# Fourteen weight slabs of an attention loop as rounded part and remainder, with reordered norms and loads

## The reference

```python
h = rms_norm(x, norm1_g[l])
z = h @ w_in[l]                                   # 1024 x 5808
(cq, ckv, kpe, gq, gk, gv, glr, gr, su, gates) = split_in(z)
o_a = mla_mixer(cq, ckv, kpe, ...)                # attention, 8 heads, two blocks of 128 queries
o_b = gla_mixer(gq, gk, gv, glr, gr, ...)         # gated linear attention
o_c = s5_mixer(su, ...)                           # y = gelu(y); y * sigmoid(y @ w_glu + b_glu)
g = sigmoid(gates + gate_b[l]).reshape(B, L, 3, D)
merged = (g[:, :, 0] * (o_a @ w_br_mla[l]) + g[:, :, 1] * (o_b @ w_br_gla[l])
          + g[:, :, 2] * (o_c @ w_br_s5[l]))
x = x + merged @ w_out[l]
h2 = rms_norm(x, norm2_g[l])
x = x + square(relu(h2 @ w_ff1[l])) @ w_ff2[l]
```

## Time and profile before

| | |
|---|---|
| median of three runs | 1526.87 us |
| profiled execution | 1527.37 us |
| its span | 1525.6 us |
| PE busy | 1479.9 us (97%) |
| PE weight loads (beside PE) | 1313.6 us (86%) |
| VectorE (DVE) busy | 739.4 us (48%) |
| ScalarE (ACT) busy | 685.2 us (45%) |
| GpSimd (POOL) busy | 862.4 us (57%) |
| mean granted TensorE clock | 0.997 of 2.4 GHz |
| loads | 234 MB, mean 154 GB/s |

### The profile page before, as it was taken

How to read it: one execution, slowest core, us unless ns; L and a number is a source line. 1 busy time by engine, 2 the same in 40 slices (tenths; PEclk the granted TensorE clock), 3 DMA queues, 4 the chain that set the end, 5 groups by cost and what they waited for, 6 DMA issues and landing times.

```text
span 1525.6 us, 23985 instructions
## 1 busy us (share of the span) xinstructions
PE 1479.9 (97%) x9775; PEld 1313.6 (86%) x9775; DVE 739.4 (48%) x1407; ACT 685.2 (45%) x1024; POOL 862.4 (57%) x364
## 2 busy tenths in 40 slices
PE   7999999999999999999999999999999999899998
PEld 6977778889898897777788888989999989799997
DVE  5978865421112697886442121128993454311112
ACT  5644222554444564422255443454445645643444
POOL 5710000878888671000086778868885536688886
PEclk9999999999999999999999999999999999999999
DMA  7633343656566563333465677656664443556664
GB/s 196 174 92 83 97 110 111 200 154 187 185 187 185 157 166 88 96 97 97 124 195 156 183 217 219 186 151 184 188 183 125 127 123 107 156 165 183 188 184 138
DMA packets 321490, 234.46 MB, mean 154 GB/s; under 512 B 9382, under 2 KB 304837, under 8 KB 321380
## 3 DMA queue, kind: packets, MB, share of 16 engines
q1 hardware_dynamic: 321380, 232.93, 52.4%
HBM read 231.82 MB, written 1.09 MB: 153 GB/s over the span
## 4 chain that ended last, share of the span: by engine, by line
PE 83%; ACT 4%; issue 4%; POOL 4%; DVE 2%; DMA 2%; SPq 0%; DVEq 0%; POOLq 0%; ACTq 0%
PE ps L678 18%; PE ps L1948 14%; PE ps L1064 7%; PE ps L1065 7%; PE ps L1066 7%; PE ps L1931 5%; PE ps L1932 5%; PE ps L1933 5%; POOL w_lo L1288 4%; DMA raw<-in_w_in_dram 1%; PE ps L1139 1%; ACT w_hi L1322 1%; PE ps L1176 1%; PE ps L2068 1%; PE ps L2082 1%
## 5 line engine op out<-in xcount | busy, mean ns | idle before, releaser
L1288 POOL TENSOR_TENSOR w_lo<-raw,w_hi 128x1024 fp32r<-128x1024 f32 (+1 forms) x206 | 490.5, 2396 | 508.2 <-ACT w_hi L1322 507.0
L746 POOL TENSOR_TENSOR w_lo<-raw,w_hi 128x1024 fp32r<-128x1024 f32 x154 | 371.7, 2421 | 144.2 <-ACT w_hi L768 142.6
L1322 ACT ACTIVATE w_hi<-raw 128x1024 fp32r<-128x1024 f32 (+1 forms) x206 | 217.5, 1058 | 239.1 <-PE ps L678 81.7
L1064 PE MATMUL ps<-h_hi,w_hi 128*128 128x256 f32 x864 | 246.3, 285 | 1.4 <-DVE h_lo L929 1.3
L1065 PE MATMUL ps<-h_lo,w_hi 128*128 128x256 f32 x864 | 244.3, 283 | 0.0
L1066 PE MATMUL ps<-h_hi,w_lo 128*128 128x256 f32 x864 | 244.2, 283 | 0.0
L1931 PE MATMUL ps<-h_hi,w_hi 128*128 128x256 f32 (+1 forms) x816 | 232.5, 285 | 4.9 <-DVE h_lo L1568 3.4
L1932 PE MATMUL ps<-h_lo,w_hi 128*128 128x256 f32 (+1 forms) x816 | 230.6, 283 | 0.0
L1933 PE MATMUL ps<-h_hi,w_lo 128*128 128x256 f32 (+1 forms) x816 | 230.5, 283 | 0.0
L768 ACT ACTIVATE w_hi<-raw 128x1024 fp32r<-128x1024 f32 x154 | 161.9, 1058 | 144.2 <-PE ps L1066 71.9
L1948 PE MATMUL ps<-hN,raw 128*128 128x256 f32 x768 | 174.9, 383 | 0.0
(11 more groups left out here) (327 smaller groups left out, 2363.1 us busy)
## 6 DMA issues: line engine op xcount, KB each, us to landing
raw<-in_w_in_dram SPq DMA_DIRECT2D x160, 512.0 KB, 3.9
raw<-in_w_ff_dram SPq DMA_DIRECT2D x128, 512.0 KB, 4.0
raw<-in_w_ffn_in_dram SPq DMA_DIRECT2D x44, 512.0 KB, 3.9
raw<-in_w_ffn_out_dram SPq DMA_DIRECT2D x22, 512.0 KB, 3.4
raw<-in_w_out_dram SPq DMA_DIRECT2D x16, 512.0 KB, 3.4
raw<-in_w_br_gla_dram SPq DMA_DIRECT2D x8, 512.0 KB, 3.5
raw<-in_w_br_mla_dram SPq DMA_DIRECT2D x8, 512.0 KB, 3.6
raw<-in_w_br_s_dram SPq DMA_DIRECT2D x8, 512.0 KB, 4.1
```

The costliest lines, as they stand in the source:

```text
L746: nc.gpsimd.tensor_tensor(out=w_lo[(NS * L + i) % RING][:, 0:kt * n], in0=raw[(NS * L + i) % RING][:, 0:kt * n], in1=w_hi[(NS * L + i) % R ...
L1064: MM(out, w[0], x[0], start=first_k, stop=False, skip_group_check=skip)
L1288: nc.gpsimd.tensor_tensor(out=w_lo[(NS * l + i) % RING][:, 0:kt * n], in0=raw[(NS * l + i) % RING][:, 0:kt * n], in1=w_hi[(NS * l + i) % R ...
L1322: A_(w_hi[(NS * l + i) % RING][:, 0:kt * n], raw[(NS * l + i) % RING][:, 0:kt * n], ACT.Copy)\
```

## The change

Fourteen slabs per layer (tiles 16 to 23 of the gates, the four of w_br_gla, the GLU's two; `in_loop`) are now rounded part and remainder too, but in buffers of their own (`wb_hi`, `wb_lo`, three each) and with the remainder on VectorE instead of GpSimd. Their right-hand sides are split as well: hN into g_hi and g_lo, rr into r_hi and r_lo, the gelu's output into u_hi and u_lo, each rounded by ScalarE and subtracted by VectorE. `raw` is let go by `wl_ok`, when the remainder is there. The square inside gelu moves from VectorE to ScalarE.

Besides: `norm_rows` takes the whole row of b = 1 at once; roundings move (`prep(I_FF + 1)` ahead of the norms, `prep(2)` ahead of a wait, one slab fewer in the second block's middle norms); the tables' load moves from behind slab I_FF + 12 to behind I_FF + 1; the bias bands come in eight loads of three rows' sets instead of four of six.

```diff
+    I_LS = I_GATE + 16
+    N_LS = I_BRA - I_LS
...
-            if b == 0:
...
+            act.wait_ge(*ready(2 * b + 1))
+            A_(sqt[:, b, :], xt[:, b, :], ACT.Square, accum_out=c[2]).then_inc(norm_sq.s, 2)
+            act.wait_ge(norm_sq.s, norm_sq(l, n + 2))
+            A_(c[3], c[2], ACT.Ln, scale=1.0 / DM, bias=C("eps")).then_inc(norm_ln.s, 2)
...
-            n = 6
+            n = 3
             band = bass.AP(scratch.tensor, 384 * n * part, [[1, P], [384, n], [1, 2 * P]])
...
-                        prep(slab + 3)
+                        prep(slab + 2)
...
-            h_rounded(1, "g_pre_ffn", J_FF + 3)
+            h_rounded(1, "g_pre_ffn", J_FF + 2)
...
+                    elif in_loop(j):
+                        sp.wait_ge(wl_ok.s, wl_ok(l, j - I_LS + 1))
                     else:
                         sp.wait_ge(used.s, used(l, j + 1))
...
-                    if i == I_FF + 12 and l == DEPTH - 1:
+                    if i == I_FF + 1 and l == DEPTH - 1:
+                        sp.wait_ge(used.s, used(l, I_OUT))
                         second_tables(sp)
...
-                    if i - I_FF in (28, 32, 36, 40) and l == DEPTH - 1:
+                    if i - I_FF in range(28, 52, 3) and l == DEPTH - 1:
...
                 norm_rows(act, A_, l, 0, 1, x_ready)
+                prep(2)
                 act.wait_ge(cols_ok.s, cols_ok(l, 1))
...
+                def loop_hi(k):
+                    i = I_LS + k
+                    if not 0 <= k < N_LS:
+                        return
+                    act.wait_ge(load_sem(l, i), load_count(l, i))
+                    if k == 2:
+                        act.wait_ge(gl_ok.s, gl_ok(l, 2))
+                    if k >= 3:
+                        act.wait_ge(used.s, used(l, i - 2))
+                    n = SLABS[i][2] * SLABS[i][4]
+                    A_(flat(i, wb_hi), raw[(NS * l + i) % RING][:, 0:n], ACT.Copy).then_inc(wh_ok.s, 1)
+
+                def gates_hi(half):
+                    act.wait_ge(of_ok.s, of_ok(l, 2))
+                    A_(g_hi[:, 4 * half:4 * half + 4, :], hN[:, 4 * half:4 * half + 4, :], ACT.Copy).then_inc(gh_ok.s, 1)
...
                 exps(0)
+                gates_hi(0)
                 for n in range(8):
...
+                    loop_hi(2 * n - 1)
                     if n < 6:
                         gate(EARLY + n)
+                    if n == 0:
+                        loop_hi(0)
                     if n + 1 < 8:
                         exps(n + 1)
+                    if n == 0:
+                        gates_hi(1)
+                    else:
+                        loop_hi(2 * n)
+                    if n == 4:
+                        act.wait_ge(y_ps.s, y_ps(l, 7))
+                        A_(r_hi, rr, ACT.Copy).then_inc(rh_ok.s, 1)
+                    if n == 5:
+                        act.wait_ge(y_rd.s, y_rd(l, 4))
+                        A_(sq[:, 4:8, :], sq[:, 0:4, :], ACT.Square, scale=float(np.sqrt(0.044715))).then_inc(ge_sq.s, 1)
...
-                prep(I_FF)
+                prep(I_FF + 1)
                 for b in range(NT):
                     norm_rows(act, A_, l, 1, b, lambda i: (x_mid.s, x_mid(l, i + 1)))
-                    prep(I_FF + 1)
...
+                def loop_lo(k):
+                    if not 0 <= k < N_LS:
+                        return
+                    i = I_LS + k
+                    n = SLABS[i][2] * SLABS[i][4]
+                    dve.wait_ge(wh_ok.s, wh_ok(l, k + 1))
+                    tt(flat(i, wb_lo), raw[(NS * l + i) % RING][:, 0:n], flat(i, wb_hi), ALU.subtract).then_inc(wl_ok.s, 1)
...
                     if h:
                         rotate(h)
+                    if n == 1:
+                        for half in range(2):
+                            dve.wait_ge(gh_ok.s, gh_ok(l, half + 1))
...
                     if n == 6:
-                        link(V.tensor_scalar(g_, g_, 0.044715, 1.0, ALU.mult, ALU.add))
-                        tt(g_, g_, y_, ALU.mult).then_inc(ge_in.s, 1)
+                        dve.wait_ge(ge_sq.s, ge_sq(l, 1))
+                        stt(g_, g_, 1.0, y_, ALU.add, ALU.mult).then_inc(ge_in.s, 1)
...
                     normalise(n)
+                    loop_lo(2 * n - 2)
...
+                    if n:
+                        loop_lo(2 * n - 1)
...
-                        product32(l, I_GATE + i, pair(u % PGF)[:, i % 2, :], 0, P, hN).then_inc(used.s, 1)
+                        if in_loop(I_GATE + i):
+                            pe.wait_ge(gl_ok.s, gl_ok(l, 2))
+                            product(l, I_GATE + i, out, 0, P, g_hi, g_lo).then_inc(used.s, 1)
+                        else:
+                            product32(l, I_GATE + i, out, 0, P, hN).then_inc(used.s, 1)
```

More of the change, by code:

```diff
@@ L240, in build @@
         xt = sb("xt", [P, NT, DM])
+        third = ExitStack()
+        wb_hi2 = sb("wb_hi2", [P, SLAB], f32r, c=third)
+        wb_lo2 = sb("wb_lo2", [P, SLAB], f32r, c=third)
+        third.close()
         hN = sb("hN", [P, KD, T])
@@ L269, in build @@
         first = ExitStack()
+        split_in = ExitStack()
+        sb("z_kept", [P, 12, T], c=split_in)
+        g_hi = sb("g_hi", [P, KD, T], f32r, c=split_in)
+        split_in.close()
         Z = sb("Z", [P, Z_TILES + 1, T], c=first)
@@ L277, in build @@
         y_lo = sb("y_lo", [P, 4, T], f32r, c=branch_in)
+        u_hi = sb("u_hi", [P, 4, T], f32r, c=branch_in)
+        u_lo = sb("u_lo", [P, 4, T], f32r, c=branch_in)
         branch_in.close()
         AR = sb("AR", [P, 8192], c=first)
-        WK = sb("WK", [P, 4608], c=first)
+        g_lo = sb("g_lo", [P, KD, T], f32r, c=split_in)
+        wb_hi = [sb(f"wb_hi{i}", [P, SLAB], f32r, c=split_in) for i in range(2)] + [wb_hi2]
+        wb_lo = [sb(f"wb_lo{i}", [P, SLAB], f32r, c=split_in) for i in range(2)] + [wb_lo2]
+        split_in.close()
+        WK = sb("WK", [P, 6144], c=first)
         o_hi = sb("o_hi", [P, 4, T], f32r, c=branch_in)
@@ L310, in build @@
         rr = MD[:, 7168:8192].rearrange("p (a t) -> p a t", a=4)
+        r_hi, r_lo = (w_lo[i][:, :].rearrange("p (a t) -> p a t", a=4) for i in (1, 0))
         kpe_g, kpe_r = fr[:, 0, 0, :], fr[:, 0, 1, :]
@@ L468, in build @@
         y_rd = sig("y_rd", 4)
+        gh_ok = sig("gh_ok", 2)
+        gl_ok = sig("gl_ok", 2)
+        wh_ok = sig("wh_ok", N_LS)
+        wl_ok = sig("wl_ok", N_LS)
+        rh_ok = sig("rh_ok", 1)
+        rl_ok = sig("rl_ok", 1)
+        uh_ok = sig("uh_ok", 1)
+        ul_ok = sig("ul_ok", 1)
+        ge_sq = sig("ge_sq", 1)
         ge_in = sig("ge_in", 1)
@@ L485, in col, with in_loop, flat, slab_parts @@
             return cols[p0:p1, at:at + 1]
+        def in_loop(i):
+            return I_LS <= i < I_BRA
+        def flat(i, part):
+            k = i - I_LS
+            return part[k % 3][:, 0:SLABS[i][2] * SLABS[i][4]]
+        def slab_parts(l, i):
+            if not in_loop(i):
+                return slab_w(l, i, w_hi), slab_w(l, i, w_lo)
+            return [flat(i, part).rearrange("p (k n) -> p k n", k=SLABS[i][2]) for part in (wb_hi, wb_lo)]
         def slab_w(l, i, part):
@@ L1846, in _ @@
                         rotate(h)
[L1847 to L1849 removed]
+                    if n == 1:
+                        for half in range(2):
+                            dve.wait_ge(gh_ok.s, gh_ok(l, half + 1))
+                            part = slice(4 * half, 4 * half + 4)
+                            tt(g_lo[:, part, :], hN[:, part, :], g_hi[:, part, :], ALU.subtract).then_inc(gl_ok.s, 1)
+                    if n == 6:
+                        dve.wait_ge(ge_sq.s, ge_sq(l, 1))
+                        stt(g_, g_, 1.0, y_, ALU.add, ALU.mult).then_inc(ge_in.s, 1)
+                    if n == 7:
+                        dve.wait_ge(ge_th.s, ge_th(l, 1))
+                        stt(y_, g_, 1.0, y_, ALU.add, ALU.mult).then_inc(of_ok.s, 1)
                     normalise(n)
+                    loop_lo(2 * n - 2)
                     if n % 2 == 0 and n:
@@ L1935, in weights @@
             def weights(l, i):
+                if in_loop(i):
+                    pe.wait_ge(wl_ok.s, wl_ok(l, i - I_LS + 1))
+                    return slab_parts(l, i)
                 if not is_split(SLABS[i]):
@@ L2032, in branch_slab @@
                     for m in range(2):
-                        last = product32(l, i, pair(4 + s)[:, m, :], P * m, P, x)
+                        last = product(l, i, pair(4 + s)[:, m, :], P * m, P, x_hi, x_lo)
                     last.then_inc(used.s, 1)
@@ L2284, in _ @@
                     for m in range(2):
-                        last = product32(l, i, pair((U_GLU + s) % PGF)[:, m, :], P * m, P, sq)
+                        last = product(l, i, pair((U_GLU + s) % PGF)[:, m, :], P * m, P, u_hi, u_lo)
                     last.then_inc(used.s, 1)
```

55 lines of the change are left out of this document (23 added, 32 removed).

## The result

The changed kernel takes 1545.32 us (median of 4 runs, 1544.89 to 1545.87) against 1526.51 of the kernel before (its three runs and a fourth): ratio 1.0119, 95% interval 1.0103 to 1.0135. It is 18.8 us slower, where the prediction had +2.4 and a range that ended at 1534. The profiled execution took 1545.00 us (before 1527.37), its span is 1543.0 us.

The account below looks back on a forecast made before the run. PE bounded the kernel before; in the changed loop VectorE's and ScalarE's order would. The loop's +5.1 us per layer (+10.2) and -7.8 outside it gave +2.4 on the profiled 1527.37, 1529.3 us with the 0.5 over the median; range 1518 to 1534.

Parts of the forecast that it names:

- Step 1: Loop's first rounded slab: ScalarE's rounding waits for its load ahead of exps(1), delaying PE's transposes of iteration 1 by 4.0 us.
- Step 2: Iterations 1 to 5: eight remainders and late roundings on VectorE add 4.8 us; transposes of iteration 5 move to 249.0.
- a rival of +3.1 for both layers: Loop: the 4 us stall at iteration 1 costs PE's clock in both layers, 1532.4 us; chance 0.13.
- Step 3: Loop's end and branches: normalise 10.3 us late at 258.5, GLU +6.9 at its end, shorter branch waits, +5.1 per layer.
- The branch's waits for w_lo: Branch behind the loop: raw slabs released earlier, so PE's waits of 0.39 and twice 0.7 go, -1.8 us per layer.
- forecast of -7.8: All edits outside the loop (tables, bands, norms, start) together gain 7.8 us, with bounds from -3 to -8.7.
- tables and bands: Layer 1's w_ff phase: moved tables' load and smaller bias bands remove PE's waits, -4.4 us; tables' share alone -2.2.
- norm2: Second norm of each layer: the second row follows at once, so h_hi comes 0.8 us earlier, twice.
- From that norm to the end: Second block's middle norms: one of two roundings leaves ScalarE's chain, -1.5 us taken.
- at the start: Kernel start: h_hi no longer behind a rounding that waited for the columns, -0.65 us.
- PE stays the bound: Rival for the loop: nothing late for PE, -11.3 us per layer and -7.8 outside, 1496.5 us; chance 0.07.
- The chances: Whole kernel against the one before: faster 0.20, same (within 0.2%) 0.42, slower 0.38.

Follow-up runs that it names:

- e3_late: The changed kernel with ScalarE's first rounded slab of the loop behind exps(1) and g_hi's second half: 1536.40 us, ratio 1.0048 to the kernel before.
- e2_warm: The changed kernel with products that nobody reads in PE's idles before its waits for p_ok: 1540.14 us, ratio 1.0069 to the kernel before.
- e5_order7: The changed kernel with VectorE's maxima(7) ahead of its remainder of the last w_br_gla slab: 1541.00 us, ratio 1.0088 to the kernel before.
- e1_outer: The kernel before with only the edits outside the attention loop: 1520.96 us, ratio 0.9943 to the kernel before.
- e11_tables: The kernel before with only the tables' load moved behind slab I_FF + 1: 1525.99 us, ratio 0.9982.
- e9_six_sq: The changed kernel with six slabs (gates fp32), Square ahead of a rounding, maxima(7) ahead of a remainder: 1511.39 us, ratio 0.9889 to the kernel before.
- e4_pool: The changed kernel with the loop's 14 remainders on GpSimd instead of VectorE: 1560.07 us, ratio 1.0194 to the kernel before.
- e10_late7sq: The changed kernel, all 14 slabs: first rounding behind exps(1), Square ahead of a rounding, maxima(7) ahead of a remainder: 1529.96 us, ratio 1.0004 to before.

## Why the prediction was wrong

The forecast named what bounds the loop rightly, and its sum was 15 us short between the spans (+2.4 against 17.4). Its steps, in its own order:

- Step 1 held to 0.2 us: the transposes of iteration 1 at 205.87 (205.7 forecast), idle 3.98 (4.0). e3_late shows that the order on ScalarE is its cause.
- Step 2 held as an arithmetic of queues: with the clock held up (e2_warm) the transposes of iteration 5 start at 249.53, forecast 249.0. It failed in what it left out. I priced the clock at one stall of a layer and put it at nothing, as a rival of +3.1 for both layers. There are three such stalls in a layer, and five of the six lowered the clock (0.76, 0.55 and 0.72 in layer 0). At the transposes of iteration 6 this is 262.08 against 259.14, 2.9 us in layer 0, and 2.2 in layer 1. A slow slab is not beside VectorE's queue, as ScalarE's row behind the slab of 5.31 shows, which let `raw` go only at 212.1:

```profile
215.88 1.06 ACT L1542 ACTIVATE wb_hi<-raw 128x1024 fp32r<-128x1024 f32 x1 [2.19 <-DMA raw<-in_w_in_dram]
```

  The load starts late, the rounding waits for it, and VectorE for the rounding (the 2.16 under e2_warm). Behind the third stall the way is through the gate's tanh.
- Step 3's head was 0.6 off (259.1 with the clock held, 258.5 forecast). Its tail is the step that failed most: from the transposes of iteration 6 to the GLU the forecast has "14.0 and needs 12.0". It measured 15.7 (262.08 to 277.81). Between them stands PE's wait for p_ex(8), exps(7). In front of exps(7) I had counted neither VectorE's two remainders of this iteration, the second with a wait of 1.37 for its rounding, nor maxima(7) behind them. PE's wait measured 1.88, and the slab behind it ran at a lower clock, 1.6 more: 3.5 a layer (27.5 - 24.0). e5_order7 shows it, and there the stretch to the GLU is 12.2, the forecast's 12.0. That I placed three operations in a row on ScalarE before gelu and didn't ask the same of VectorE before exps(7) is the mistake.
- Layer 0: 5.1 forecast, 2.9 for the clock of the stalls, 3.5 for the wait for exps(7) with its slow slab, and 1.2 of small differences at either end give 12.7. Layer 1: 5.1, 2.2, 3.5 and 0.8 give 11.6. The small differences have no run of their own.
- The branch's waits for w_lo fell from 0.39, 0.41 and 0.63 to one of 0.26. That gave 1.5 us to the third slab instead of the forecast 1.8: its first two slabs take 6.0 (283.56 to 289.58) instead of 7.1, and the first has no wait.
- Outside the loop the forecast of -7.8 held: -7.9 by the medians of e1_outer, -6.9 in the profiled execution of the changed kernel. In that execution tables and bands give -4.5 (-4.4 forecast; the shift to before falls from 22.6 at 838.32, the first w_ff1 product, to 18.0 at 1022.17, the next norm), split as forecast by e11_tables, and norm2 -0.8 each, as forecast. From that norm to the end it is -0.6 instead of -1.5, but -1.6 in e1_outer, where the 32 transposes took 5.47; at the start the executions differ by more than the forecast 0.65. Neither can be told from one trace.
- The rival "PE stays the bound" needs VectorE's work gone: in the loop PE runs without a wait for p_ok only where the gates were left out (e9_six_sq). The rival of the lost clock had the right mechanism; it counted one stall a layer, and the stalls cost 5.1 for both layers instead of 3.1.
- The chances were added up wrongly: by the rivals' own figures faster is 0.18 and slower 0.40, not 0.20 and 0.38.

What stays open is when the clock falls. The windows behind the three idles of layer 1:

```profile
710.70:717.00 6.30, 6.25 (x41) 5.38 (x42) 5.04 (x9) 3.08 (x8) 0.00 (x0) 1.00 0.08 15
732.80:739.00 6.20, 6.19 (x41) 5.89 (x42) 4.62 (x8) 2.24 (x5) 0.00 (x0) 0.73 0.49 138
754.30:760.00 5.70, 5.63 (x27) 5.63 (x28) 4.84 (x8) 2.60 (x4) 0.00 (x0) 0.50 0.36 107
```

The first, of 3.52, has 1.00 behind it, those of 3.25 have 0.73 and 0.50, and in layer 0 one of 1.88 has 0.79 and one of 1.73 has 1.00. The length of the idle alone doesn't decide, and the same stall is not always priced the same: the 3.25 before iteration 5 of e3_late leaves the four transposes at 1.12 in layer 0 and at 0.66 in layer 1. No run was made for it.

## What to carry to other kernels

A stall of the bound engine can be priced twice: its length, and what the engine does more slowly behind it. Ask this of every stall, and follow what waits for the slow work, a buffer that it releases late or a result that the other engine's queue stands behind: by these ways the second price got into the queue that caused the first, 1.4 and 1.3 us here, while a third was almost hidden. When work is put into the queue of a second engine, go through every wait of the bound engine and ask what now stands ahead of its releaser, a rounding that waits for a load above all. And take the part of a change that fits into the idle engine's slack: six slabs of 14, in the right order, gave some 8 us in the loop where all 14, as first ordered, cost 24.

## What the hardware showed unexpectedly

- VectorE stands still beside a GpSimd operation on SBUF (e4_pool): 2.21 us instead of 0.17 for a tensor_scalar of two columns, 6.31 instead of 2.43 for four scans, while GpSimd keeps its 2.35 to 2.39.
- PE's clock fell behind idles of 3.25 us and of 1.88 us in the loop, and stayed at 1.00 behind one of 3.52.
- Behind one and the same idle of 4.2 us, 32 transposes took from 5.47 (e1_outer, e9_six_sq) to 6.45 us (e10_late7sq). A gain of under 1 us beside such an idle can't be read from one trace.
